# Expert 0 is sorted like the other fifteen, the router product is turned round, and ranks are taken by comparing all pairs

## What is computed

```
scores = sigmoid(t @ w_router)                                   # 256 x 16
biased = (scores + router_bias).reshape(-1, 4, 4)                # 4 groups of 4 experts
group_score = top_k(biased, 2)[0].sum(-1)
gidx = top_k(group_score, 1)                                     # the best group alone
eidx = top_k(where(group is gidx, biased, -inf), 2)              # 2 experts in it
w = sel / sel.sum(-1)                                            # of their unbiased scores
for e in range(16):
    he = silu(t @ w_gate[e]) * (t @ w_up[e])                     # 1024 x 512 each
    y = y + combine[:, e] * (he @ w_down[e])                     # 512 x 1024
```

## Time and profile before

| | before |
|---|---|
| median of 3 runs | 2167.6 us (2164.62 to 2170.58) |
| profiled execution | 2172.88 us, its span 2171.1 us |
| PE busy in the span | 2026.2 us |
| DVE busy | 831.8 us |
| ACT busy | 377.4 us |
| mean granted clock of PE | 0.965 of full speed |

### The profile page before, as it was taken

How to read it: one execution, slowest core, us unless ns; L and a number is a source line. 1 busy time by engine, 2 the same in 40 slices (tenths; PEclk the granted TensorE clock), 3 DMA queues, 4 the chain that set the end, 5 groups by cost and what they waited for, 6 DMA issues and landing times.

```text
span 2171.1 us, 41363 instructions
## 1 busy us (share of the span) xinstructions
PE 2026.2 (93%) x18924; PEld 1761.5 (81%) x18924; DVE 831.8 (38%) x1432; ACT 377.4 (17%) x693; POOL 14.9 (1%) x10
## 2 busy tenths in 40 slices
PE   6989879989999898978999999999999999999999
PEld 4778668889999687767889999666888788888878
DVE  4767674300001856853310000476576402123310
ACT  3021322000001112241100001326111101011100
POOL 0000000000000000000000000000000000000000
PEclk9989988999999999989999999999999999999999
DMA  9992546289997473426269999120488544434420
GB/s 360 387 357 75 194 151 241 78 333 356 404 396 294 155 255 108 176 97 231 83 240 365 395 392 394 69 78 1 160 303 278 209 155 154 147 123 149 140 83 20
DMA packets 184180, 466.06 MB, mean 215 GB/s; under 512 B 5152, under 2 KB 55680, under 8 KB 176384
## 3 DMA queue, kind: packets, MB, share of 16 engines
q1 hardware_dynamic: 183776, 463.83, 58.5%
q10 hardware_dynamic: 288, 0.52, 0.1%
HBM read 463.29 MB, written 1.05 MB: 214 GB/s over the span
## 4 chain that ended last, share of the span: by engine, by line
PE 85%; DVE 9%; ACT 2%; DMA 2%; issue 1%; SPq 0%; DVEq 0%; ACTq 0%
PE pair L360 83%; DVE AR L1495 2%; DMA ring<-in_ada_w 2%; PE pair L991 1%; ACT AR L1223 1%; DVE AR L1712 1%; DVE RST L1550 1%; DVE XH L1495 0%; DVE AR L1722 0%; PE pair L614 0%; SPq L251 0%; PE pair L861 0%; DVE AR L1726 0%; DVE AR L1798 0%; DVE AR L1804 0%
## 5 line engine op out<-in xcount | busy, mean ns | idle before, releaser
L360 PE MATMUL pair<-AR,ring 128*64 128x96 f32 (+1 forms) x12992 | 812.6, 262 | 29.5 <-issue 15.7
L360 PE MATMUL pair<-XH,ring 128*128 128x256 f32 (+4 forms) x3584 | 815.1, 389 | 22.0 <-ACT XH L1126 16.1
L360 PEld LDWEIGHTS pair<-AR,ring 128*64 128x64 f32 (+1 forms) x12992 | 763.7, 144 | 76.6 <-issue 22.8
L360 PEld LDWEIGHTS pair<-XH,ring 128*128 128x128 f32 (+3 forms) x3584 | 683.4, 192 | 138.4 <-issue 31.4
L1965 DVE TENSOR_TENSOR AR<-AR,pair 128x384 f32<-128x384 f32 x30 | 16.6, 554 | 450.6 <-PE pair L360 450.6
L1495 DVE SCALAR_TENSOR_TENSOR AR<-ring,CACT,AR 128x512 f32<-128x512 f32 x245 | 184.2, 752 | 8.7
L360 PE MATMUL pair<-AR 128*64 128x128 f32 (+5 forms) x768 | 107.0, 338 | 8.7 <-ACT AR L1393 3.3
L1582 DVE SCALAR_TENSOR_TENSOR XH<-pair,MOD,XH 128x256 f32<-128x256 f32 x64 | 28.3, 480 | 214.6 <-PE pair L360 214.5
L360 PEld LDWEIGHTS pair<-AR 128*64 128x64 f32 (+3 forms) x768 | 79.9, 170 | 21.6 <-ACT AR L1393 4.1
L2063 DVE SCALAR_TENSOR_TENSOR AR<-pair,VEC,AR 128x255 f32<-128x255 f32 x88 | 41.9, 476 | 114.9 <-ACT AR L1418 114.9
L1328 ACT ACTIVATE AR<-pair 128x768 f32 x30 | 24.5, 815 | 305.7 <-PE pair L360 305.7
(11 more groups left out here) (250 smaller groups left out, 1116.5 us busy)
## 6 DMA issues: line engine op xcount, KB each, us to landing
ring<-in_ada_w SPq DMA_DIRECT2D x48, 2048.0 KB, 12.7
ring<-in_w_gate SPq DMA_DIRECT2D x32, 2048.0 KB, 9.1
ring<-in_w_up SPq DMA_DIRECT2D x32, 2048.0 KB, 9.4
ring<-in_w_down SPq DMA_DIRECT2D x32, 2048.0 KB, 9.3
ring<-in_ffn_w_up SPq DMA_DIRECT2D x44, 1024.0 KB, 7.5
ring<-in_w_in SPq DMA_DIRECT2D x18, 2048.0 KB, 13.3
ring<-in_ffn_w_down SPq DMA_DIRECT2D x8, 2048.0 KB, 7.9
ring<-in_sc_w_in SPq DMA_DIRECT2D x6, 2048.0 KB, 8.0
```

Source lines behind the costliest of these rows:

```text
L360: return pe.matmul(o, lhsT, rhs, start=start, stop=stop, **kw)
```

## The change

Expert 0 joins the sorted list: `CNT`, `OFF` and the masks have 16 entries where they had 15, its three dense products and `broadcast(0)` go (they remain in the overflow branch alone), and `c_gate`, `c_up`, `c_down` run for e = 0 too, e = 0 reading its window straight from `XS`. The first chunks of a layer are loaded in the order gate 0, up 0, gate 1, up 1, down 0. The gather goes half of the tokens by half over all eight PSUM banks, so that the first half can start when the first `PERM` is there. The router's product has `WR` as the stationary operand, widened to 32 columns with zeros; tile t of eight goes to columns 32 (t mod 4) of the array, four partial sums stand below each other in PSUM, DVE copies them out, and two small products with `GATHER` add the four and turn them. `rank` compares each of four values with each other in one instruction, where equal values count by a triangle `LOWER`. `YS` is no longer cleared by POOL.

```diff
             sp.dma_start(CS[:, C_U:C_U + P], T["before"]).then_inc(s["slots_in"], 16)
-            sp.dma_start(WR[:, :, :], T["w_router"].rearrange("(t p) n -> p t n", p=P)).then_inc(s["router_in"], 16)
+            sp.wait_ge(s["wr_zero"], 1)
+            sp.dma_start(WR[:, :, 0:NE], T["w_router"].rearrange("(t p) n -> p t n", p=P)).then_inc(s["router_in"], 16)
...
-                for m in range(2):
-                    for t in range(KT):
-                        if m == 0:
-                            h_tile(n, t)
-                        last = mm(PD[:, 512 + NE * m:512 + NE * m + NE], H1[:, t, m * P:m * P + P], WR[:, t, :],
-                                  t == 0, t == KT - 1)
-                last.then_inc(s["rt_ready"], 1)
+                for t in range(KT):
+                    h_tile(n, t)
+                    j = 32 * (t % 4)
+                    last = mm(PD[j:j + 32, 512:512 + S], WR[:, t, :], H1[:, t, :], t < 4, t >= 4)
+                last.then_inc(s["rt_part"], 1)
...
+                h_turned(0)
+                pe.wait_ge(s["rt_copied"], l + 1)
+                pe.wait_ge(s["gather_ready"], 1)
+                for m in range(2):
+                    last = mm(PD[:, 768 + NE * m:768 + NE * m + NE], LOGIT[:, m * P:m * P + P], GATHER[:, :], True, True)
+                last.then_inc(s["rt_ready"], 1)
+                h_turned(1)
...
-                gate(m0, 0, wait=False)
...
-                pe.wait_ge(s["ht_ready"], l + 1)
-                up(m0 + 1, 0, wait=False)
-                broadcast(0)
...
+                pe.wait_ge(s["ht_ready"], 2 * l + 2)
+                for m in range(2):
+                    pe.wait_ge(s["perm_ready"], 2 * l + m + 1)
+                    for t in range(KT):
+                        last = mm(xbank(t), HT8[m][:, t, :], PERM[m], m == 0, m == 1, skip_group_check=True)
+                        if m == 1:
+                            last.then_inc(s["xs_ready"], 1)
...
-                down(m0 + 2, 0)
...
-                    c_gate(m0 + 3, 1)
-                    c_up(m0 + 4, 1)
-                    c_gate(m0 + 5, 2)
-                    c_up(m0 + 6, 2)
-                    c_down(m0 + 7, 1)
-                    c_gate(m0 + 8, 3)
-                    c_up(m0 + 9, 3)
-                    c_down(m0 + 10, 2)
+                    c_gate(m0, 0)
+                    c_up(m0 + 1, 0)
+
+                    pe.wait_ge(s["placed_ready"], 2 * l + 2)
+                    for k in range(4):
+                        for m in range(2):
+                            last = pe.transpose(PC[:, S * k + P * m:S * k + P * m + P], PLACED[m][:, k * P:k * P + P], ident)
+                    last.then_inc(s["st_turned"], 1)
+                    for e in range(1, 4):
+                        c_gate(m0 + 3 * e - 1, e)
+                        c_up(m0 + 3 * e, e)
+                        c_down(m0 + 3 * e + 1, e - 1)
...
                 norm(2 * l + 1, X1, H1, 0, l, 1)
+                V.wait_ge(s["rt_part"], l + 1)
+                V.tensor_copy(LOGIT, PD[:, 512:512 + S]).then_inc(s["rt_copied"], 1)
                 V.wait_ge(s["rt_sig"], l + 1)
...
-                    link(V.memset(rk, 0.0))
-                    for d in range(1, n):
-                        lo, hi = val[:, :, 0:n - d], val[:, :, d:n]
-                        g_ = ge[:, :, 0:n - d]
-                        link(V.tensor_tensor(g_, lo, hi, ALU.is_ge))
-                        link(V.tensor_tensor(rk[:, :, d:n], rk[:, :, d:n], g_, ALU.add))
-                        link(V.tensor_scalar(g_, g_, -1.0, 1.0, ALU.mult, ALU.add))
-                        link(V.tensor_tensor(rk[:, :, 0:n - d], rk[:, :, 0:n - d], g_, ALU.add))
...
+                    step(V.tensor_tensor(gt, vj, vi, ALU.is_gt))
+                    link(V.tensor_tensor(ge, vj, vi, ALU.is_ge))
+                    link(V.tensor_tensor(ge, ge, low, ALU.mult))
+                    link(V.tensor_tensor(gt, gt, ge, ALU.max))
+                    link(V.tensor_reduce(rk.rearrange("p (q i) -> p q i", q=q), gt, axis=AXX, op=ALU.add))
...
-                pool.memset(YS, 0.0).then_inc(s["ys_zero"], 1)
```

More of the change, by code:

```diff
@@ L701, in gate @@
                         pe.wait_ge(s["sg_ready"], i * 2 + (16 * l + e))
-                    done(features(c, [half(PA, m) for m in range(4)], hk if e == 0 else hp, i=i))
+                    done(features(c, [half(PA, m) for m in range(4)], hp, i=i))
                 def up(c, e, i=0, wait=True):
@@ L706, in up @@
                         pe.wait_ge(s["gu_ready"], i * 2 + (16 * l + e))
-                    done(features(c, [half(PB, m) for m in range(4)], hk if e == 0 else hp, i=i))
+                    done(features(c, [half(PB, m) for m in range(4)], hp, i=i))
                 def down(c, e, i=0, parity=0):
@@ L779, in _ @@
                     pe.wait_ge(s["hp_ready"], l + 1)
-                    for g in range(1, 4):
+                    for g in range(4):
                         broadcast(g)
                     pe.wait_ge(s["cbc_copied"], 4 * l + 4)
-                    gate(m0 + 3, 1)
-                    up(m0 + 4, 1)
+                    gate(m0, 0, wait=False)
+                    up(m0 + 1, 0, wait=False)
+                    gate(m0 + 2, 1)
+                    up(m0 + 3, 1)
+                    down(m0 + 4, 0)
                     with pe.Fori(0, 7) as i:
@@ L1330, in c_outputs @@
                           ACT.Copy).then_inc(s["ys_copied"], 1)
-                    c_silu(1)
-                    for e in range(2, NE):
+                    c_silu(0)
+                    act.wait_ge(s["st_turned"], l + 1)
+                    A(blk(12), PC, ACT.Copy).then_inc(s["st_copied"], 1)
+                    for e in range(1, NE):
                         c_silu(e)
@@ L1479, in _ @@
                 link(V.tensor_scalar(LB[:, 1, l, :], LB[:, 0, l, :], -1.0, 1.0, ALU.mult, ALU.add))
+            link(V.memset(LOWER[:, :, :], 0.0))
+            for i in range(1, 4):
+                ins = V.memset(LOWER[:, i, 0:i], 1.0)
+            ins.then_inc(s["lower_ready"], 1)
+            V.wait_ge(s["const1_in"], 16)
+            V.tensor_reduce(GATHER[:, :], ident.rearrange("p (j i) -> p i j", j=4)[:, 0:NE, :], axis=AXX, op=ALU.add)\
+                .then_inc(s["gather_ready"], 1)
             COS, SIN = RT[64:96, 0:S], RT[64:96, S:2 * S]
@@ L1901, in _ @@
                 for m in range(2):
-                    step(V.tensor_scalar(PERM[m], IOTA, PLACE[:, m:m + 1], None, ALU.is_equal))
-                settle()
-                for m in range(2):
+                    link(V.tensor_scalar(PERM[m], IOTA, PLACE[:, m:m + 1], None, ALU.is_equal))
                     V.scalar_tensor_tensor(PERM[m], IOTA, PLACE[:, 2 + m:3 + m], PERM[m], ALU.is_equal, ALU.add)\
```

200 lines of the change are left out of this document (90 added, 110 removed).

## The result

| | before | changed |
|---|---|---|
| median | 2168.5 us (4 runs) | 2114.4 us (4 runs, 2108.3 to 2116.3) |
| ratio | | 0.9746, 95% interval 0.9718 to 0.9773 |
| profiled execution | 2172.9 us, span 2171.1 | 2116.3 us, span 2114.5 |

With a fourth run the median before is 2168.5, where it was 2167.6 of three. The change takes 54 us off, where 38 were forecast; the time lies under the range. I measure each layer's mixture part from the start of the router's first product to the start of ACT's last copy of a sorted expert's output. It was 319.1 us in layer 0 and 319.3 in layer 1, and is 657.08 - 365.65 = 291.4 now, and 291.5 in layer 1. The rest of the kernel is as long as it was, within 1 us.

A forecast was written before the change was run, and what follows sets the result against it. PE was taken as the bound, busy 93% of the span. Per layer, 37.65 us gained up to the first sorted product minus 18.55 added behind it gave 19.1, 38.2 for two; 2167.6 became 2129.5 us, range 2118 to 2142.

The forecast's parts named there:

- T: Start of layer 0's first sorted product on PE, forecast at 398.85 us, 37.65 us earlier than 436.50.
- Steps 1 to 3: Router product, DVE copy with 8 transposes at 0.21, `GATHER` products and sigmoid: sigmoid done at 372.3 us, before 373.45.
- Step 4: Selection on DVE: 15 instructions, five wide ones at 0.32; 3.7 us in all, bounds 3.0 and 4.3, done at 376.0.
- Step 5: Places on PE, ten rows after an idle stretch: 2.0 us, bounds 1.2 and 2.4, done at 378.0.
- Step 6: DVE from the places to the first half's `PERM`: 2.0 plus 1.25 us, ready at 381.25.
- Step 7: Gather on PE, 32 rows: 13.90 us as before plus 2.5 for the low clock, ending at 397.65.
- Step 8: PE's branch after the gather: the first sorted product waits 1.20 us, as after the last transposes before.
- Behind T: Sorted part: three added chunks at straight code's 5.84 plus transposes 1.04, 18.55 us together; the rest keeps 248.8.
- only 348 GB/s: First sorted stretch: DMA moved 348 GB/s, later 392, so late chunks were put down to instructions, 0.56 us a chunk.
- The cheap rival: Chunks at 5.28, clock up at once, selection and places at lower bounds: 5.7 more a layer, 2118 us; 17%.
- a given-back gain: Rival: with expert 0 at a third of its time, the weight stream bounds the kernel; 2167 us, 3%.
- an overflow: Rival: expert 0 has more than 96 tokens in a layer, so all 16 experts run for all tokens; 2533 us, 2%.

The follow-up runs named there:

- e7: Changed kernel with the old router product (H1 blocks stationary, 16 columns moving) and all 16 transposes behind it: 2124.5 us, ratio 0.9809 to the kernel before.
- e6: Changed kernel with the old `rank` put back (26 instructions in place of 10): 2123.4 us, ratio 0.9798 to the kernel before.
- e9: Changed kernel with three filler products of constants in each of PE's two idle stretches ahead of the gather: 2115.1 us, ratio 0.9762 to the kernel before.
- e5: Changed kernel with the 8 transposes of `PLACED` put back ahead of PE's branch: 2120.9 us, ratio 0.9782 to the kernel before.
- e14: Kernel before with the 8 transposes of `PLACED` moved into the middle of expert 0's dense down product: 2164.2 us, ratio 0.9988.
- e1: Changed kernel loading only half of each sorted weight chunk from gate 2 on, PE's work unchanged: 2100.6 us, ratio 0.9678 to the kernel before.
- e2: Changed kernel with PE's loop over experts 4 to 15 written out: 2154.1 us, ratio 0.9930 to the kernel before.
- e4: Kernel before with the weight chunk issued 2 us ahead of the first sorted product held until the first sorted chunk is through: 2167.1 us, ratio 0.9992.
- e11: Kernel before loading only half of each weight chunk from gate 2 on: 2150.9 us, ratio 0.9916.

## Why the prediction missed the size

The mechanism was right in the large: the dense matrices go, the routing lies bare, three sorted chunks are added. Of the 55.6 us that both mixture parts lost in the traces 17.4 were not forecast, most of them because two costs of the kernel before, the gap at the branch and late chunks, were carried over as if they belonged to the code. By its own steps, in layer 0, from the router's start (T forecast at 32.7, measured at 29.0):

- **Steps 1 to 3, router.** Forecast 6.1 us to the end of the sigmoid, measured 5.0 (365.65 to 370.66). I had kept the low clock for the transposes (0.21 each, measured 1.09 / 8 = 0.14), but it ended by 370; e7 shows that it was the old router that held it down. Mis-sized by 1.1.
- **Step 4, selection.** Forecast 3.7 with 0.32 per wide instruction; measured 3.5 and 0.29 (the first wide instruction). Right.
- **Step 5, places.** Forecast 2.0, measured 1.36 from the first product to the copy (1.5 from the end of the selection): full clock. Mis-sized by 0.5. (In e6 and in layer 1 of several runs it took 2.29 at the low clock.)
- **Step 6, `PERM`.** Forecast 3.25, measured 3.3 from the copy to the second instruction's end. Right.
- **Step 7, gather.** Forecast 16.4, measured 15.6 to the first sorted product; 1.8 lost to the clock where I took 2.5. Right within its bounds; e9 confirms the cause.
- **Step 8, branch.** Forecast 1.20, measured 0. Wrong: I took the gap as a cost of the branch that goes with it. The first product comes some 4.4 us behind the flag's load at the earliest, and the gap is only what the array's queue leaves of that (e5, e14).
- **Behind T.** Forecast 248.8 + 18.55 = 267.4, measured 262.4. This is the largest miss, 5.0 a layer. The term was "3 x 5.84", with "the rest keeps its 248.8". First, the 248.8 held a late first chunk, 7.75 for 5.54, which the changed kernel does not have: 2.2. Second, "straight code costs 0.56 a chunk" is not so: code is late only while weights stream (e1), and the 16 intervals took 5.67 and not 5.84, 2.7 us. The first three of them came on time (15.97 us in all) and the other 13 took 5.75 each. That the idle DMA before them had let the fetch run ahead would fit, but is not shown.

Per layer that is 3.7 + 5.0 = 8.7, twice 17.4. So the step that failed most is the price behind T, and the one that had its cause wrong is step 8. I had the rows for the branch in hand: the flag's load has a row of its own and I did not look at it. And where I took DMA load as proof that the DMA was not the cause ("only 348 GB/s"), I excluded the weights alone and not the code that shares the engines with them.

The rule of the Trainium skill, "Runtime: NRT & Kernel Launch", section "Instruction fetch mechanics", that the fetch is hidden, holds in e1 (5.28 in straight code) and not with weights streaming (e2, 5.9 and more). Its warning of the taken branch is borne out with 4.4 us. The cheap rival, with chunks at 5.28 and the clock up at once, gave 2118: the nearest of mine, and still short, for it kept the gap and the first chunk as well. That it came so near is luck: the 16 intervals took 5.67, the clock cost the gather 1.8 us and the selection took 3.5, not its lower bound of 3.0; of its four terms only the places came near. That a given-back gain or an overflow would decide did not come up: no dense product stands behind the gather, and PE waits nowhere for weights.

## What to carry to other kernels

Before a cost of the kernel before is kept in the sum, ask what it hangs on: a gap after a branch hangs on what is queued ahead of it, so put long instructions and not short ones there, and look for the row in which the sequencer loads its condition. A PE that waits for "issue" beside a DMA at its limit may be waiting for its own code: see whether instruction packets land just ahead of its restarts. If so, keep the code in a loop, start the loop early, and don't write loops out while weights stream. When dense work that hid a chain goes, each instruction of that chain is worth its full time, and shortening it in the same edit is what makes the edit whole (taken back alone, they cost 9 us in e6 and 10 in e7, about half of the 10 as late code behind it).

## What the runs showed that I had not expected

- The time from the load of a flag to the first PE product behind the branch was 4.2 to 4.8 us in five kernels (before, e4, e5, e11, e14), where the queue did not cover it.
- PE's sequencer was 17 product rows ahead of the array at the branch: 7.7 us over the gather's rows of 0.43 us, and 3.2 us when 8 transposes stood last.
